# Hybrid decoder layer: output projection by token chunks, norms chunk by chunk, decode values in four column groups

## The reference

```python
out_a = gelu(gr) * hr                                  # (tokens, 512), recurrence
o = einsum('btngs,btsnd->btngd', p, vg)                # attention values; decode: over the pages
mix = concatenate([rms_norm(out_a, gn_lru_g), rms_norm(out_b, gn_att_g)], -1) @ w_out
x = x + g1[:, None, :] * mix
h2 = modulate(rms_norm(x, ln2_g), sh2, sc2)
ff = (silu(h2 @ w_gate) * (h2 @ w_up)) @ w_down        # 2816 wide
x = x + g2[:, None, :] * ff
```

## Time and profile before

| | |
|---|---|
| median of 3 runs | 1687.61 us (1684.68 to 1690.97) |
| profiled execution | 1686.55 us, span 1684.8 us |
| TensorE busy | 1434.9 us, 85% |
| VectorE busy | 743.0 us, 44% |
| ScalarE busy | 550.8 us, 33% |
| GpSimd busy | 334.0 us, 20% |
| DMA | 103.41 MB, mean 61 GB/s |
| granted TensorE clock, mean | 0.909 |

### The profile page before, as it was taken

The page is one execution under the profiler, slowest core; times in us unless marked ns, Lnnn a source line. Parts: engine busy times, 40 slices in busy tenths (PEclk is TensorE's granted clock), DMA queues, the critical chain, the costliest instruction groups (busy, mean ns, idle before and its releaser), DMA issues.

```text
span 1684.8 us, 23362 instructions
## 1 busy us (share of the span) xinstructions
PE 1434.9 (85%) x8679; PEld 1290.2 (77%) x8679; DVE 743.0 (44%) x1555; ACT 550.8 (33%) x835; POOL 334.0 (20%) x201
## 2 busy tenths in 40 slices
PE   4878989965127899969955899999999999999997
PEld 3656989923015565758945899999999999999997
DVE  3856787499766562243134022303223033131334
ACT  3546878523257674321122111111111111111112
POOL 0340201199200000011200122121211221222110
PEclk8988999967568999869977999999999999999999
DMA  9511101092100000224100111111111211111102
GB/s 364 163 32 38 51 25 26 20 363 87 44 19 8 1 1 18 61 72 138 38 25 13 38 50 39 39 53 49 51 39 38 63 39 49 50 42 45 50 13 101
DMA packets 115561, 103.41 MB, mean 61 GB/s; under 512 B 15527, under 2 KB 99823, under 8 KB 115088
## 3 DMA queue, kind: packets, MB, share of 16 engines
q1 hardware_dynamic: 114416, 98.00, 18.3%
q10 hardware_dynamic: 1056, 4.19, 0.7%
HBM read 92.36 MB, written 9.85 MB: 61 GB/s over the span
## 4 chain that ended last, share of the span: by engine, by line
PE 68%; DVE 13%; issue 9%; ACT 4%; ACTq 2%; DVEq 2%; SPq 1%; POOL 0%; DMA 0%; POOLq 0%
PE ps L1950 13%; PE ps L1952 12%; PE ps L1951 12%; PE ps L2141 4%; PE ps L2143 4%; PE ps L2142 4%; PE ps L2034 2%; PE ps L2022 2%; DVE score L1119 2%; ACTq L872 2%; PE ps L2100 2%; PE ps L2012 2%; ACT junk L870 1%; PE ps L2013 1%; PE ps L2073 1%
## 5 line engine op out<-in xcount | busy, mean ns | idle before, releaser
L685 POOL TENSOR_TENSOR wL<-wraw,wH 128x1024 fp32r<-128x1024 f32 x82 | 196.6, 2405 | 1172.0 <-ACT wH L863 592.7
L1950 PE MATMUL ps<-h2H,wH 128*128 128x344 f32 x1056 | 340.6, 323 | 41.0 <-ACTq L1075 29.6
L1951 PE MATMUL ps<-h2L,wH 128*128 128x344 f32 x1056 | 339.4, 321 | 0.0
L1952 PE MATMUL ps<-h2H,wL 128*128 128x344 f32 x1056 | 339.1, 321 | 0.0
L1950 PEld LDWEIGHTS ps<-h2H,wH 128*128 128x128 f32 x1056 | 200.6, 190 | 42.3 <-issue 42.3
L1683 DVE TENSOR_TENSOR af<-ps,sg 128x1032 f32<-128x1032 f32 x22 | 27.1, 1233 | 465.5 <-PE ps L1952 465.5
L1119 DVE SCALAR_TENSOR_TENSOR xT<-ps,mod,xT 128x344 f32<-128x344 f32 (+2 forms) x280 | 161.1, 581 | 124.7 <-PE ps L1952 69.8
L1951 PEld LDWEIGHTS ps<-h2L,wH 128*128 128x128 f32 x1056 | 200.7, 190 | 0.0
L1952 PEld LDWEIGHTS ps<-h2H,wL 128*128 128x128 f32 x1056 | 200.7, 190 | 0.0
L2141 PE MATMUL ps<-aH,wH 128*128 128x344 f32 x480 | 153.8, 320 | 0.0
L2143 PE MATMUL ps<-aH,wL 128*128 128x344 f32 x480 | 153.2, 319 | 0.0
(11 more groups left out here) (373 smaller groups left out, 2666.6 us busy)
## 6 DMA issues: line engine op xcount, KB each, us to landing
adb<-in_ada_w SPq DMA_DIRECT2D x8, 2048.0 KB, 8.0
wraw<-in_w_gate SPq DMA_DIRECT2D x22, 512.0 KB, 3.9
wraw<-in_w_up SPq DMA_DIRECT2D x22, 512.0 KB, 3.9
wraw<-in_w_down SPq DMA_DIRECT2D x22, 512.0 KB, 3.7
x_feature_major<-x0T SPq DMA_DIRECT2D x1, 4128.0 KB, 13.2
ada_scale<-in_ada_w ACTq DMA_DIRECT2D x2, 2048.0 KB, 15.3
xin<-in_x_prompt SPq DMA_DIRECT2D x8, 512.0 KB, 17.1
ada_shift<-in_ada_w SPq DMA_DIRECT2D x2, 2048.0 KB, 11.6
```

The lines of the kernel that those rows point to most:

```text
L685: pool.tensor_tensor(wL[s][:], wraw[s][:], wH[s][:].bitcast(F32), ALU.subtract).then_inc(s_wL, 1)
L1950: mm(dst, wH[s][:, k, :], hi[:, k, cc], start=(k == 0), stop=False)
L1951: mm(dst, wH[s][:, k, :], lo[:, k, cc], start=False, stop=False)
L1952: ins = mm(dst, wL[s][:, k, :], hi[:, k, cc], start=False, stop=(k == KD - 1))
```

## The change

**The projection by token chunks.** There are three chunks of 384, 384 and 264 tokens, and for each of them all eight weight slices: 24 groups of 24 matmuls in place of 8 units of 72. The weights of the projection are thus loaded, cast and subtracted three times. Five PSUM banks take the groups in turn.

**Group norms.** The squares of a group are added on VectorE, and one product with ones sums them. The scaling works in place in `gel` and `attT`, by chunk and by half (recurrence blocks, attention blocks). The mix of the 8 sample tokens' attention half is done apart, later. The sums of the recurrence group stand behind the key pages of the third sequence, those of the attention group behind the last logits.

**Second norm.** ScalarE squares each block of a chunk as its residual is added, VectorE adds the squares (`square_added`), and one product with ones sums them (`sums2`), two groups into the next chunk. The norm of a chunk is made while the next one is projected. After the last group TensorE does six sub-units of the first two FFN slices (`first_units`), in the order of the chunks, so that the tokens of chunks 0 and 1 come first.

**Decode values.** The V page is the moving operand (128 columns), and 32 columns of probabilities the stationary one; four sequences use four groups of 32 columns of the array. The result is copied out and transposed back. The V pages of sequences 4 to 7 are loaded during attention.

**Order.** The decode query transposes come behind the score product, and `qb` is cleared behind them. Projection group 0 stands before the probability transposes, group 1 before the values, group 2 before the back transposes. Buffers move; among them `xT` lies where decode buffers lay, so five of its blocks come back only after the back transposes.

The core of the diff:

```diff
+OUT_CHUNKS = ((0, 384), (384, 384), (768, 264))
+OUT_PROMPT = (384, 384, 256)
+OUT_BANKS = (5, 6, 0, 1, 2)
+NU_LRU, NU_OUT = 8, 24
...
 (SyncE)
-            sp.wait_ge(s_hd, NG)
-            for b in range(2, NB):
-                pages(vpg, "cache_v", s_vpg[b // 2], b)
+            sp.wait_ge(s_out, 16 * 5)
+            for b in range(4, NB):
+                pages(vpg, "cache_v", s_ivp[b // 2], b)
             sp.wait_ge(s_hd, NG)
             sp.dma_start(xT[:, 0:3, :], spill[:, 0:3, :]).then_inc(s_xback, 16)
+            for b in range(2, 4):
+                pages(vpg, "cache_v", s_ivp[b // 2], b)
+            for g in range(SLOTS):
+                sp.wait_ge(s_dkt, g + 1)
+                load_out(g)
+            for g in range(SLOTS, 6):
+                load_out(g)
+            sp.wait_ge(s_dvt, 1)
             sp.dma_start(xT[:, 3:KD, :], spill[:, 3:KD, :]).then_inc(s_xback, 16)
+            for g in range(6, NU_OUT):
+                load_out(g)
...
 (ScalarE)
+            for n in range(LT):
+                group_square(n)
+            for b in range(4):
+                page_keys_out(b)
+                group_square(LT + b)
+            group_root(0)
+            page_keys_out(4)
+            high(U_OUT)
+            page_keys_out(5)
+            page_keys_out(6)
+            high(U_OUT + 1)
+            page_keys_out(7)
+            for n in range(LT):
+                mix_high(0, n)
+            group_root(1)
+            high(U_OUT + 2)
             act.wait_ge(s_dmx, 1)
             A(dlg[:], dlg[:], ACT.Exp, ...)
+            for n in range(LT, KD):
+                mix_high(0, n)
+            high(U_OUT + 3)
...
+            squared(2)
+            high(U_OUT + 6)
+            for n in range(LT, KD):
+                mix_high(2, n)
             act.wait_ge(s_dat, 4)
+            A(gss[:], attT[:, NTT, :, 0:NB], ACT.Square).then_inc(s_gsq, 1)
...
+            for g in range(4, NU_OUT):
+                c, n = g // KD, g % KD
+                squared(g)
+                if g < NU_OUT - 1:
+                    high(U_OUT + g + 4)
+                if c >= 1 and n == 1:
+                    root2(c - 1)
+                if c >= 1 and 3 <= n < 7:
+                    for d in range(2 * n - 6, 2 * n - 4):
+                        normed2_high(c - 1, d)
...
 (VectorE)
+            squares_added(0, NTOK)
+            dve.wait_ge(s_gsu, 1)
+            group_variance(nr[0][:, 0:T], wide_sum)
...
+            V.reciprocal(nr[0][:], nr[0][:])
+            squares_added(1, T)
+            mix_half(0, 0)
+            dve.wait_ge(s_gsu, 2)
+            group_variance(nr[1][:, 0:T], wide_sum)
...
+            V.reciprocal(nr[1][:, 0:T], nr[1][:, 0:T])
             dve.wait_ge(s_dlg, NB + 1)
...
             V.tensor_scalar(dsm[:, 1:2], dsm[:, 0:1], -SCALE, None, ALU.mult).then_inc(s_dmx, 1)
+            mix_half(0, 1)
             dve.wait_ge(s_dex, 1)
...
+            for g in range(6, NU_OUT):
+                c, n = g // KD, g % KD
+                residual(g)
+                square_added(g - 1)
+                if c >= 1 and n == 1:
+                    variance2(c - 1)
+                if c >= 1 and n == 2:
+                    root_inverse(c - 1)
+                if c >= 1 and 3 <= n < 7:
+                    d = 2 * n - 6
+                    normed2(c - 1, d)
+                    normed2(c - 1, d + 1)
+                    dve.drain()
+                    normed2_low(c - 1, d)
+                    normed2_low(c - 1, d + 1)
...
 (TensorE)
+            out_group(0)
             pe.wait_ge(s_dpn, 1)
...
+            out_group(1)
             pe.wait_ge(s_dpe, 1)
-            mm(ps[:, 0, 0:64], vt[0:NB, NTT, :], ptl[:], start=True, stop=False, skip_group_check=True)
-                for g in range(PG):
-                    ins = mm(ps[:, 0, 8 * b:8 * b + 8], vpg[b][:, g, :], dpT[:, g, 8 * b:8 * b + 8],
...
+            for r in (0, 1):
+                for q in range(4):
+                    b = 4 * r + q
+                    mm(ps[32 * q:32 * q + 32, 4, r * P:(r + 1) * P], ptl[:, 8 * b:8 * b + 32], vnew[:],
+                       start=True, stop=False, skip_group_check=True)
...
+                for g in range(PG):
+                    for q in range(4):
+                        b = 4 * r + q
+                        ins = mm(ps[32 * q:32 * q + 32, 4, r * P:(r + 1) * P],
+                                 dpT[:, g * 64 + 8 * b:g * 64 + 8 * b + 32], vpg[b][:, g, :],
+                                 start=False, stop=(g == PG - 1), skip_group_check=True)
+            out_group(2)
...
+            out_group(3)
+            out_group(4)
+            pe.wait_ge(s_gsq, 2 * LT + 1)
+            for c in range(LT):
+                ins = mm(ps[:, 7, 0:NB], ones, gss[:, c, :], start=(c == 0), stop=(c == LT - 1))
+            ins.then_inc(s_gsu, 1)
+            for g in range(5, NU_OUT):
+                out_group(g)
+                if g >= KD and g % KD == 1:
+                    sums2(g // KD - 1)
+            def first_units():
+                for q, (k0, c) in enumerate(((0, 0), (0, 1), (1, 0), (1, 1), (0, 2), (1, 2))):
...
+                    if q == 1:
+                        sums2(2)
```

More of the change, by code:

```diff
@@ new lines, in _ @@
+            for n in range(LT):
+                mix_high(2, n)
+            squared(2)
+            high(U_OUT + 6)
+            for n in range(LT, KD):
+                mix_high(2, n)
+            act.wait_ge(s_dat, 4)
+            A(gss[:], attT[:, NTT, :, 0:NB], ACT.Square).then_inc(s_gsq, 1)
+            squared(3)
+            high(U_OUT + 7)
+            group_root(2)
+            act.wait_ge(s_gt, 3 * KD + 1)
+            nc.scalar.copy(mixH[:, LT:KD, T:NTOK], attT[:, NTT, :, 0:NB]).then_inc(s_gH, 1)
@@ L1657, in sample_residual @@
+            for d in range(KD):
+                if d + 1 < KD:
+                    dve.drain()
+                    normed2(2, d + 1)
+                normed2_low(2, d)
+            dve.drain()
             def sample_residual(gate_at, src):
@@ L1773, in ada_columns @@
                 ins.then_inc(s_modk, 1)
-            def stats(src, ready, used, b0, n, first=0, per=1):
-                for d in range(n):
-                    pe.wait_ge(ready, per * (first + d + 1))
-                    for c in range(NCH):
-                        ins = mm(ps[:, b0 + c, 0:CW], ones, src[(first + d) % 2][:, c * CW:(c + 1) * CW],
-                                 start=(d == 0), stop=(d == n - 1))
-                    ins.then_inc(used, 1)
             pe.wait_ge(s_dg, 1)
@@ L2075, in decode_logits, with group_sums @@
                 ins.then_inc(s_dlg, 1)
+            def group_sums(grp):
+                pe.wait_ge(s_gsm, grp + 1)
+                if grp == 0:
+                    pe.wait_ge(s_dqe, 2)
+                    mm(ps[:, 3, 0:NB], ones, gsq[:, 0, T:NTOK], start=True, stop=True)
+                else:
+                    pe.wait_ge(s_gv, 1)
+                for hf in range(2):
+                    ins = mm(ps[:, 6 + hf, :], ones, gsq[:, LT * grp, hf * HT:(hf + 1) * HT], start=True, stop=True)
+                ins.then_inc(s_gsu, 1)
             pe.wait_ge(s_dqe, 1)
@@ L2119, in gate_up @@
                 n2 = i * 4 if i is not None else 0
[L2120 removed]
+                for k in range(2 if b == 0 else 0, 4):
                     pe.wait_ge(s_wL, n12 + (u + k + 1))
                     pe.wait_ge((s_sg, s_af)[k % 2], n2 + (2 * b + k // 2 + 1))
[L2124 removed]
+                    unit(u + k, h2H, h2L, 3 * (k % 2))
             def down(u, par, b, i=None):
```

470 lines of the change are left out of this document (296 added, 174 removed).

## The result

The changed kernel takes **1642.24 us** (median of 4 runs, 1639.09 to 1643.48), the kernel before 1686.14 beside it (1681.99 to 1690.97). The ratio is 0.973 (0.9702 to 0.9758): faster by 44 us, where I had forecast 75. The time is outside my range of 1596 to 1632.

The account below looks back on a forecast made before the run. TensorE, with two chains of VectorE in its path, was taken as the bound. The steps move the end of FFN units 0 and 1 from 925.5 to 850.2, saving 75.3 of 1687.61 us: 1612, range 1596 to 1632.

Parts of the forecast that it names:

- Step 1: Decode logits, 660 to 695 us: +2.6 for the first key page, +1.9 for group sums, about 0.9 wait; end 695.2.
- step 5: The 19 projection groups left: 69.4 us, two sums of 0.7, and +3 from the ring, ending at 827.1.
- Step 2: Attention group's norm chain on VectorE: projection group 0 waits 14 us for the first attention block; group 1 ends at 723.5.
- Step 3: Decode value products: 8.5 us where 27.5 stood, ending at 732.0.
- rival B: Value products: column groups don't overlap, +9.5 us, 1622, or +26, 1638, at the low clock; chance 0.10.
- Step 4: Before group 5: TensorE waits 6.4 us behind the large x transfer, until 751.3, plus 2 us for the clock.
- the ring: Second norm, narrow chunk: VectorE waits for ScalarE, whose cast waits for TensorE; 4.15 against 2.95 us, four groups, leaving +3.
- Step 6: Norm of chunk 2: 13.4 us beside 15.6 of TensorE work, so nothing waits; units 0 and 1 end at 850.2.
- 773 us of FFN unchanged: Expected sign: the FFN, 773 us from 912 us to the end before, stays the same except for its start.
- A: Rival: the waits of steps 2, 4 and 5 are partly filled, giving 1599 us; chance 0.15.
- C: Rival: the weight stream bounds the projection groups, 5.15 us each, 98 for 72.4, giving 1637 us; chance 0.10.
- D: Rival: the weight stream makes it slower than before, 19 groups taking 148 us, 7.8 each; chance 0.03.

Follow-up runs that it names:

- the memsets: Changed kernel with GpSimd's low part of the w_out weights replaced by two memsets, so left out of the projection: 1624.12 us, 0.9643.
- The version with the divided reciprocal: Changed kernel with the reciprocal of the attention group's norm in two parts, 384 columns first: 1635.54 us, 0.9716.
- the spread version: Changed kernel with two earlier weight loads, second reciprocal in two parts, 13 low parts on VectorE, second norm spread thinner, ScalarE copies earlier, sub-units reordered: 1621.81 us, 0.9625.
- a shift of 256: Changed kernel with 256 already met waits at the start of TensorE's program: 1644.8 us (one run).
- a shift of 128: Changed kernel with 128 already met waits at the start of TensorE's program: 1632.0 us (one run).
- The spread and shifted version: The spread version with 128 already met waits at the start of TensorE's program: 1606.94 us, 0.952 to the kernel before.
- the shifted versions: Changed kernel with 64, 128, 192 or 256 already met waits at TensorE's start: 1647.0, 1632.0, 1631.3, 1644.8 us (one run each).

## Why the prediction was wrong, by its own steps

**Step 1, decode logits: right in size, one term missed.** They end near 697.5, which is my 695.2 and the 2.1 us by which attention ended later in this profile. Behind them one VectorE addition (L1655) took 3.37 us, with 1.23 for its neighbours, beside a GpSimd subtraction (692.98 to 695.88): +2.1, the same cause as in step 5. With the memsets group 0 goes on 2.1 us earlier in the stretch.

**Step 2, the new wait: right.** 13.2 us for my 14. The version with the divided reciprocal shows that the 6.6 us reciprocal is part of it: 9.2 is left.

**Step 3, values: right in kind, sized too high.** 4.5 us for my 8.5, which I had built on the 0.05 us of the earlier trace rows. In turns an instruction takes 0.030 us, in one group 0.093: rival B is refuted. The Trainium skill, "TensorE: Matmul & The Clock Gate", Part 3, "The mechanism", lets weight loads overlap only where the row group differs. Here all share their rows and differ in columns, and the order of the columns alone makes 8 us: the measurement decides against the rule.

**Step 4, reload of x: right as a sum, by luck.** Group 5 starts at 750.96, where I had 751.3. But the late attention and the addition (+4.2) and the values (-4.0) cancel in it. The wait was 4.5 us and not 6.4, and group 5 ran at a granted clock of 0.59 (750.96 to 757.80), for which I had added 2 us.

**Step 5 is the step that failed: "the ring takes residual 0.95, square 0.45, cast 1.05, two copies 1.1, subtraction 0.6, about 4.15 against 2.95 us, in four groups; some 2 us of slack go first, leaving +3".** It was 5.7 us, and in eight groups: four of the narrow chunk, against 2.9 of TensorE, and four of the wide chunk before it (residuals at 792.5, 798.2, 803.8 and 809.5), against 4.21, where I had looked for no ring. The first of each four came even 8.6 and 7.2 us behind the residual before it. The subtractions were priced alone and took 3.0 us a pair beside GpSimd's. I had GpSimd's 2.39 in the sum as a stage of the weight slot, and never as something beside which VectorE stops. What that cost: waits of 8.1 and 9.3 us and the low clock after each, +7.5 to the end of the groups and +12.5 behind it. The memset version takes 12.6 of these 20.0 us away (and 3.2 ahead of the sample sums), though its last three pairs still take 3.0. The wait of 6.4 us that is left behind them is 1.8 in the spread version, which changes both, the subtractions and the order.

The Trainium skill, "SBUF — State Buffer", "SBUF: two separate sides", says that an operation of VectorE with two inputs in SBUF and a reading one of GpSimd exclude each other for the whole instruction. Rows 851.14 to 853.64 of before and 789.23 to 792.50 of after agree for two inputs. With one input on GpSimd the stop was not whole: 1.62 us beside a pass of 2.88. The copy from PSUM at 851.35 was not held up.

**Step 6, the cover of the last norm: wrong for the same reason.** "So nothing waits" held for chunk 2's own chain, but VectorE reached it late: TensorE waited 9.3 us before the first sub-unit, for a residual. In the spread version the cover holds but for 1.8 us and the small waits per block.

**"773 us of FFN unchanged": wrong by 10.1 us, 9.1 of them in the loop.** The work is unchanged, the loop's place in TensorE's stream is not. I took a stretch that the diff doesn't touch as untouched. The Trainium skill, "Runtime: NRT & Kernel Launch", "Instruction fetch mechanics", says that instructions come in blocks of 16 KiB, 256 instructions, one after the other, and that TensorE's instruction memory holds 2048 of them. The runs agree with the blocks (transfers of 16 KB, the same stalls at a shift of 256). The page also says that a taken branch whose target lies outside the current window of two blocks waits for a transfer. Read so for TensorE, every return of this loop would stall; with a shift of 128 only one of four did, so the measurement decides against that reading. By the page's 2048 an estimate for the body, 864 products a pass at two instructions each and the waits, would fill 7 to 8 blocks of 8, so whether it is held would hang on where it begins; no run here shows what is held.

**Rivals.** A did not come. C, a bound by the weight stream, would have spaced all groups by 5.15; the wide ones ran at 4.21 until 800. D would have taken 7.8 us a group, which none of them came near.

The account: +2.1 attention, +2.1 the addition before step 2, -4.0 values, -0.5 steps 2 and 4, +7.5 and +12.5 behind group 5 (groups, then FFN start) make +19.7; with +10.1 for the rest of the FFN, 9.1 of it in the loop, it is +29.8. The +2.1 of attention is how this profile fell. Of the 20.0 behind group 5 the memset and the spread version take 12.6 each, counted from the start of the sample sums to the end of units 0 and 1 (120.5 us after, 107.9 in both). The 7.4 us that stay above my forecast are not all explained: in the spread version 4.4 of them are the four waits named there. The spread and shifted version shows most of both causes removed.

## What to carry to other kernels

When work of VectorE moves beside GpSimd, look in the trace for an operation with two SBUF inputs that was already stretched there, and price every operation that reads two SBUF tiles beside a GpSimd one that does too as one after the other; if GpSimd takes 2.4 us for what VectorE does in 1.2, giving it back to the busier engine can be the faster choice. A stretch in which an engine had no reason to contend before can have one once two chains share it. An edit ahead of a long hardware loop moves the loop: compare the idle time at its returns and the instruction transfers before judging the edit, and try a shift of met waits.

## What was not expected of the hardware

- 64 instructions (32 float32 products of 128 columns with 32-column weights): 1.95 us when the four column groups take turns, 5.96 one group after the other.
- VectorE, a pair of 384 columns with two SBUF inputs, beside a GpSimd operation of 1024 columns: 2.88 to 3.04 us with two GpSimd inputs, 1.5 to 1.7 with one, 1.15 beside a memset.
- A return of TensorE's loop costs nothing or 4.4 us (5.7 to 6.9 in some of the shifted versions). Shifts of 0, 64, 128, 192 and 256 waits gave 4, 4, 1, 2 and 4 stalls; each goes with 9 transfers of 16 KB.
